# Two decoder layers on one core: the query projection is made from rows that carry only the norm's weights, and the token's factor comes in at the copy

## The reference

```python
def reference(...):
    for l in range(DEPTH):
        ...
        dp, st_p = mixer(rmsnorm(xp, norm_mix[l]), prm, None)
        ds, st_s = mixer(rmsnorm(xs, norm_mix[l]), prm, past)
        xp = xp + dp
        xs = xs + ds
        xp = xp + channel_mixer(rmsnorm(xp, norm_ffn[l]), l, ...)
...
def mixer(h, prm, past):
    (q, kc, vc, ks, vs, kw, vw, g_nsa, u, o_pre, if_pre, g_a, g_b) = split_cols(h @ prm['w_in'])
    q = q.reshape(b, t, NSA_KV_HEADS, NSA_GROUP, HEAD_DIM) * (HEAD_DIM ** -0.5)
    ...
    conv_prev = past['conv']
```

## Time and profile before

| what | us |
|---|---|
| median of 3 runs | 1853.33 (1851.79 to 1854.4) |
| the profiled execution, its own time | 1854.55 |
| its span in the profile | 1852.9 |
| TensorE busy in the span | 1746.0 (94%) |
| VectorE busy | 1035.3 (56%) |
| ScalarE busy | 810.8 (44%) |
| chain that ended last, share of TensorE | 85% |

### The profile page before, as it was taken

The page is one execution under the profiler, slowest core; times in us unless marked ns, Lnnn a source line. Parts: engine busy times, 40 slices in busy tenths (PEclk is TensorE's granted clock), DMA queues, the critical chain, the costliest instruction groups (busy, mean ns, idle before and its releaser), DMA issues.

```text
span 1852.9 us, 22952 instructions
## 1 busy us (share of the span) xinstructions
PE 1746.0 (94%) x8548; PEld 1394.4 (75%) x8548; DVE 1035.3 (56%) x1189; ACT 810.8 (44%) x873; POOL 176.7 (10%) x237
## 2 busy tenths in 40 slices
PE   6999979997999989998999899999999999999997
PEld 4567667777999956766776578888888888888875
DVE  2043421615454212343143468888888888888887
ACT  2013331114343110333120357777777767676764
POOL 2222011210000042201121010000000000000020
PEclk9999988998999989999899789999999999999999
DMA  8348323172554455521416389999999999999993
GB/s 239 122 156 253 112 67 93 52 229 63 165 180 163 90 163 183 159 69 58 103 46 214 134 301 332 401 351 400 356 402 350 400 352 403 352 395 360 393 391 122
DMA packets 230152, 424.92 MB, mean 229 GB/s; under 512 B 32414, under 2 KB 127934, under 8 KB 229884
## 3 DMA queue, kind: packets, MB, share of 16 engines
q1 hardware_dynamic: 217244, 383.62, 59.2%
q0 software_dynamic: 12832, 40.28, 6.6%
HBM read 403.70 MB, written 24.29 MB: 231 GB/s over the span
## 4 chain that ended last, share of the span: by engine, by line
PE 85%; DVE 6%; DMA 4%; ACT 2%; issue 2%; DVEq 0%; POOLq 0%; POOL 0%; SPq 0%; ACTq 0%
PE ps L717 81%; PE ps L721 4%; DMA weights_in<-in_moe_w 2%; DVE weights_low L1725 2%; DVE arena L1725 2%; ACT weights_high L1343 1%; DMA out_s_conv<-arena 1%; DVE arena L1912 1%; DMA arena<-in_cache_win 0%; DVE arena L1739 0%; DMA arena<-in_vecs 0%; POOLq L2415 0%; DMA arena<-in_state_conv 0%; DVE arena L1742 0%; DVE ffn_low L1725 0%
## 5 line engine op out<-in xcount | busy, mean ns | idle before, releaser
L717 PE MATMUL ps<-arena 128*128 128x288 f32 (+20 forms) x3180 | 719.9, 384 | 32.9 <-DMA arena<-in_vecs 8.9
L717 PEld LDWEIGHTS ps<-arena 128*128 128x128 f32 (+7 forms) x3180 | 508.9, 183 | 224.6 <-issue 91.5
L1725 DVE TENSOR_TENSOR weights_low<-weights_in,weights_high 128x3072 fp32r<-128x3072 f32 (+1 forms) x192 | 589.2, 3088 | 108.6 <-ACT weights_high L1343 108.4
L1343 ACT ACTIVATE weights_high<-weights_in 128x3072 fp32r<-128x3072 f32 (+1 forms) x192 | 489.6, 2560 | 200.2 <-PE ps L717 173.0
L717 PE MATMUL ps<-weights_high,item_high 128*128 128x512 f32 x704 | 279.2, 397 | 7.9 <-DVE weights_low L1725 7.2
L717 PE MATMUL ps<-weights_low,item_high 128*128 128x512 f32 x704 | 275.5, 391 | 0.0
L717 PE MATMUL ps<-weights_high,item_low 128*128 128x512 f32 x704 | 275.5, 391 | 0.0
L1340 ACT ACTIVATE arena<-arena 128x128 f32<-128x128 f32 (+12 forms) x188 | 74.9, 413 | 290.6 <-DVE arena L1725 95.8
L717 PEld LDWEIGHTS ps<-weights_high,item_high 128*128 128x128 f32 x704 | 133.3, 189 | 37.0 <-DVE weights_low L1725 9.6
L1343 ACT ACTIVATE arena<-ps 128x512 f32<-128x512 f32 (+16 forms) x146 | 63.3, 463 | 211.3 <-PE ps L721 136.6
L717 PEld LDWEIGHTS ps<-weights_high,item_low 128*128 128x128 f32 x704 | 133.1, 189 | 28.2
(11 more groups left out here) (182 smaller groups left out, 1438.1 us busy)
## 6 DMA issues: line engine op xcount, KB each, us to landing
weights_in<-in_moe_w SPq DMA_DIRECT2D x192, 768.0 KB, 8.1
weights_in<-in_moe_w SPq DMA_DIRECT2D x48, 1536.0 KB, 9.5
weights_in<-in_moe_w SPq DMA_DIRECT2D x64, 512.0 KB, 5.0
ffn_in<-in_ffn_w SPq DMA_DIRECT2D x30, 1024.0 KB, 7.1
weights_in<-in_moe_w SPq DMA_DIRECT2D x16, 1024.0 KB, 9.0
arena<-in_w_in SPq DMA_DIRECT2D x32, 384.0 KB, 4.0
arena<-in_w_in SPq DMA_DIRECT2D x32, 256.0 KB, 5.0
token_slots<-arena SPq DMA_DIRECT2D x12, 512.0 KB, 6.3
```

The source lines that it names most:

```text
L717: return nc.tensor.matmul(out, lhsT, rhs, start=start, stop=stop)
L1343: return nc.scalar.activation(out, x, ACT.Copy, scale=scale)
L1725: return V.tensor_tensor(out, x, y, op)
```

## The change

The query projection no longer reads `hT`. VectorE writes weighted rows `xg[k] = xT[k] * weight[k]`, without the token's factor, and TensorE makes the query tiles from them. The factor `srow` is multiplied in when VectorE, no longer ScalarE, copies the four query tiles out of PSUM. In layer 0 the eight weighted tiles are made just ahead of the norm, in layer 1 each one right after its residual addition at the end of the SwiGLU. On TensorE query tile 0 comes first, then the sums of the norm, then tiles 1 to 3, then the transposes of the convolution state, now into bank 7. The first key and value tile is what waits for `hT` now. ScalarE copies the state out after the square root, and takes the square root's table earlier by a one-column square root (`warm_m`): ahead of the squares in layer 0, after unit 33 for layer 1.

```diff
+        xg = take(KD * N, work0 + 2048).rearrange("p (k n) -> p k n", k=KD)
@@ tensor, start of a layer
-                pe.wait_ge(cvp_in.sem, cvp_in.at(l))
                 if l == 0:
                     pe.wait_ge(bp_ev.sem, bp_ev.at(0))
                     pe.wait_ge(vt_ev0.sem, vt_ev0.at(0))
                 else:
                     pe.wait_ge(fy_ev.sem, fy_ev.at(0))
-                for h in range(MH):
-                    m = tr(ps[:, 1, h * 24:h * 24 + 24], cvp[0:24, h * P:h * P + P])
-                m.then_inc(cv_pe.sem, 1)
-                norm(2 * l, 0 if l == 0 else KD - 2, KD)
-
                 pe.wait_ge(wl[0].sem, mixer_in(l, 0))
                 w = pslot(0, KD, 512)
                 for g in range(G):
                     if g == 1:
-                        pe.wait_ge(cv_ev.sem, cv_ev.at(l))
+                        norm(2 * l, 0 if l == 0 else KD - 2, KD)
                     for k in range(KD):
                         if g == 0:
-                            pe.wait_ge(h_ev.sem, h_ev.at(2 * l, k + 1))
-                        m = mm(ps[:, g, 0:N], w[:, k, g * P:g * P + P], hT[:, k, :], k == 0, k == KD - 1)
+                            pe.wait_ge(xg_ev.sem, xg_ev.at(l, k + 1))
+                        m = mm(ps[:, g, 0:N], w[:, k, g * P:g * P + P], xg[:, k, :], k == 0, k == KD - 1)
                     m.then_inc(q_pe.sem, 1)
+                pe.wait_ge(cvp_in.sem, cvp_in.at(l))
+                for h in range(MH):
+                    m = tr(ps[:, 7, h * 24:h * 24 + 24], cvp[0:24, h * P:h * P + P])
+                m.then_inc(cv_pe.sem, 1)
@@ tensor, key and value tiles
                         if b < 2:
                             pe.wait_ge(q_ev.sem, q_ev.at(l, b + 1))
+                        elif b == 7:
+                            pe.wait_ge(cv_ev.sem, cv_ev.at(l))
                         for k in range(KD):
+                            if f == 0 and m == 0:
+                                pe.wait_ge(h_ev.sem, h_ev.at(2 * l, k + 1))
@@ scalar, norm, after the square root
+                act.wait_ge(cv_pe.sem, cv_pe.at(idx // 2))
+                copy(uext[:, :, T + 3:UE].rearrange("p h (b x) -> p h b x", b=NB)[:, :, :, 0:3],
+                     ps[:, 7, 0:96].rearrange("p (h b x) -> p h b x", h=MH, b=NB)).then_inc(cv_ev.sem, 1)
@@ scalar, start of a layer
+                if l == 0:
+                    fn(warm_m, c("eps"), ACT.Sqrt)
                 norm(2 * l, fy_ev if l == 1 else None, 6 * l)
-                act.wait_ge(cv_pe.sem, cv_pe.at(l))
-                copy(uext[:, :, T + 3:UE].rearrange("p h (b x) -> p h b x", b=NB)[:, :, :, 0:3],
-                     ps[:, 1, 0:96].rearrange("p (h b x) -> p h b x", h=MH, b=NB)).then_inc(cv_ev.sem, 1)
-                for g in range(G):
-                    act.wait_ge(q_pe.sem, q_pe.at(l, g + 1))
-                    copy(qT[:, g, :], ps[:, g, 0:N], HD ** -0.5).then_inc(q_ev.sem, 1)
@@ scalar, end of layer 0's SwiGLU
                         unit_high(u)
+                        if u == 33:
+                            fn(warm_m, c("eps"), ACT.Sqrt)
@@ vector, start of a layer
+            def rows_weighted(l, k):
+
+                V.tensor_scalar(xg[:, k, :], xT[:, k, :], vT[:, V_MIX + 8 * l + k:V_MIX + 8 * l + k + 1], None, ALU.mult
+                                ).then_inc(xg_ev.sem, 1)
+
             for l in range(2):
                 dve.wait_ge(vt_ev0.sem, vt_ev0.at(0))
+                if l == 0:
+                    for k in range(KD):
+                        dve.wait_ge(xt_ev.sem, xt_ev.at(0, k + 1))
+                        rows_weighted(0, k)
                 norm(2 * l, V_MIX + 8 * l)
+                for g in range(G):
+                    dve.wait_ge(q_pe.sem, q_pe.at(l, g + 1))
+                    V.scalar_tensor_tensor(out=qT[:, g, :], in0=ps[:, g, 0:N], scalar=HD ** -0.5, in1=srow,
+                                           op0=ALU.mult, op1=ALU.mult).then_inc(q_ev.sem, 1)
@@ vector, end of layer 0's SwiGLU, tiles 0 to 5 and again tiles 6 and 7
                                 tt(xT[:, d, :], xT[:, d, :], ps[:, YBANK[d % 4], 0:N], ALU.add).then_inc(fy_ev.sem, 1)
+                                dve.drain()
+                                rows_weighted(1, d)
```

More of the change, by code:

```diff
@@ L401, in build @@
         cvp_in, cmp_in = ev("conv_in", 16), ev("cmp_in", 16 * 34)
[L402 to L406, removed]
+        q_pe, cv_pe, kv_pe, u_pe, o_pe, if_pe, ct_pe, kt_pe, hid_pe, mqk_pe, kc_pe = ev("mixer_tensor", 41).steps(
+            4, 1, 6, 4, 4, 1, 9, 1, 2, 8, 1)
+        xg_ev, q_ev, kv_ev, u_ev, cst_ev, uc_d, if_ev, qz_ev = ev("mixer_vector", 26).steps(8, 4, 6, 4, 1, 1, 1, 1)
+        cv_ev, gs_ev, o_ev, uc_a, ct_a, kt_ev, lf_a, lf_a2, row_a, hid_ev, kc_a = ev("mixer_scalar", 19).steps(
+            1, 1, 4, 1, 5, 1, 1, 1, 1, 2, 1)
         lf_d, ct_d, lf_d2, row_d, c_ev, mqk_ev, hidr_ev, kc_d = ev("compress_vector", 19).steps(1, 4, 1, 1, 2, 8, 1, 1)
@@ L2136, in _ @@
                         tt(xT[:, d, :], xT[:, d, :], ps[:, YBANK[d % 4], 0:N], ALU.add).then_inc(fy_ev.sem, 1)
-                    dve.drain()
+                        dve.drain()
+                        rows_weighted(1, d)
                 else:
```

## The result

The changed kernel's median was 1839.8 us (1834.14 to 1843.34, four executions) against 1853.87: a ratio of 0.9923, 95% interval 0.9896 to 0.9950. It is faster, by 14.1 us where 18.5 were forecast, and the median stands 0.3 us above the stated range. The profiled execution was the fastest of the four, 1834.14. Three more calls timed the same kernel: 1837.0, 1836.95 and 1839.51, six executions each, against medians of the kernel before of 1854.12, 1854.55 and 1855.52 in the same calls. So the gain was 14.1, 17.1, 17.6 and 16.0 us by call, and the median of all 22 executions is 1838.3. Eight of the 22 lie above 1839.5, the upper end of the range.

What follows compares the result with a forecast made beforehand. TensorE was taken to bound the kernel, losing time to waits and slow clock at both layers' starts. Gains 5.4 + 13.1 = 18.5 us gave 1836.05 for the profiled execution, 1834.8 against the median; range 1831.5 to 1839.5.

Steps and rivals of the forecast that it cites:

- The bound and the place: TensorE, 85% of the chain; its waits at both layers' starts: normed tiles 7.5 us, convolution state 5.8 us.
- rivals 2 and 3: Window cache waits: layer 0's gain ends there, 1840.2, 8%; or both layers' gains do, no change, 1853.3, 4%.
- Rival 4: Layer 1's start: query weights arrive late, beyond a 1.8 us margin; slower past 18.5 us of lateness; 3%.
- Rival 5: Layer 1's first matmul still waits for `fy_ev`, so the 5.1 us would stay: 1839.9; no chance of its own.
- Layer 1, 13.1 us: SwiGLU's end to first key matmul, 678.24 to 665.1: 3.76 pause, 5.1 transfer, rest slow clock.
- Layer 0, 5.4 us: Layer 0's start: first key matmul moves from 60.36 to 55.0, a gain of 5.4 us.
- 55.0: Layer 0's first key matmul: start 35.2, then 3.88 tile 0, 3.88 sums, 11.64 tiles 1 to 3, 0.40 transposes.
- my 0.42: Weighted tile on VectorE: 0.42 us, taken between rows of 0.406 (one operand) and 0.511 (two operands).
- Parts at nothing: Both layers: norm chain, four query copies on VectorE, SwiGLU's weighted tiles and earlier table load cost nothing, being covered.
- The sum: 18.5: Both layers' starts: 5.4 + 13.1 = 18.5 us, carried to the end unchanged.
- with 1.5 us either way for the spread between runs (2.6 us before): Whole kernel: margin around the forecast 1834.8, also for half-clock stretches elsewhere that shift; the forecast had 70%.
- the clock rival: Layer 0's start: clock falls all the same as the pause grows from 1.99 to about 2.6; costs up to 1.96 us; 15%.

## Why the prediction was partly right

**The bound and the place: right.** The waits named are the ones that went, and only they. The window cache's waits stayed at 9 us each, so rivals 2 and 3 fall. Rival 4 falls: the first query matmul of layer 1 starts 0.51 us after the addition begins, so the weights were there. Rival 5 falls with it. (Rival 4's price for a landing at 670 us comes to 1856.6, not 1856: 1834.8 + 670 - 648.24.)

**Layer 1, 13.1 us: right.** Start to first key copy went from 36.0 to 23.2, which is 12.7 us unrounded, and it is 23.2 in all four profiles of the full change; alone layer 1 gave 13.8 on the median.

**Layer 0, 5.4 us: right in mechanism, 5.0 in size, less when the clock falls.** Alone it gave 4.5 on the median. From the end of the setup's matmuls (32.64 before, 33.13 after) to the first key copy it took 33.0 us before and 28.0 after, so 5.0; the same 28.0 stands in the three profiles of the full change that held the clock, and 29.4 in the one where it fell. From weighted tile to key matmul the pair of profiles shows 35.62 + 19.64 + 0.35 = 55.6 where I had 55.0; the setup itself ended half a microsecond later in that execution. The weighted tile took 0.33 us on the path and 0.371 on the mean, under my 0.42 and its lower end of 0.406.

**Parts at nothing: right.** Norm chain, query copies (0.452 against 0.454), weighted tiles and table load stayed under cover; the copies' last one ends 5.5 us before VectorE's next work.

**The sum: 18.5, a little too large; measured 14.1 at first and 16 to 17.6 later.** The two starts give 5.0 + 12.7 = 17.7 in the profiles. The missing 0.8 lies in two terms. The prediction took the start of ScalarE's copy (60.36, 678.24) for the first key matmul; the records of the kernel before have 396-column matmuls from 60.1 and 678.0 on, so each gain was counted 0.2 us too large. And a query tile takes 3.93 us (19.64 / 5), not 3.88. From 17.7 to the full change's pooled 16.2 (1854.5 less 1838.3) or, by means, 16.8 (1854.8 less 1838.0) no second cost was found, and none is needed: resampling the 65 and 22 executions puts the medians' difference between 14.5 and 18.9 us. In one profile of four the fall at layer 0's start takes 1.4 us. Elsewhere the pieces move both ways: layer 1's mixer has 389.1 to 393.3 us against 390.1 before, the experts and the end 773.6 to 779.4 against 777.0 and 779.2, and the fastest of the four executions has a mixer of 392.3. How much of the last microsecond the change brings and how much is chance is open.

**What failed is the step "with 1.5 us either way for the spread between runs (2.6 us before)".** Three executions stood for the spread. Calls with 21, 17, 11 and 11 executions of the kernel before spread over 11.5, 8.9, 8.1 and 10.2 us, and the changed kernel over 9 in its first four. The same three executions set the base of the sum, 1853.33, where 65 executions have 1854.5: the forecast stood 1.2 us low by that, and 2.3 by a gain of 16.2 in place of 18.5. So the changed kernel's centre, 1838.3, is 3.5 us above 1834.8, inside the range but near its upper end. Medians of four drawn from the 22 executions go from 1834.6 to 1841.5 in 95 of 100 draws, and about one in four lies above 1839.5. That the first one did is bad luck; that it could is the failed step. The same step left the clock rival too small: 15% and 1.96 us, against three falls in six profiles with the new pause (one in four of the full change), of up to 3.0 us. Its reason, that the pause grows from 2.0 to 2.6 us, is not borne out: the clock fell after the old pause too, in two of five. The Trainium skill (TensorE: Matmul & The Clock Gate, Part 1) says of its own measurements that the point of change varies from run to run. I cited it for the rival's direction and didn't draw its consequence for the range.

## What to carry to other kernels

A factor of the token can be taken out of the moving rows and put in where the tile is copied out of PSUM: the matmuls then start without the norm, and the norm's chain hides under them. Look for a second wait in front of the same place (here the state's transfer), since each alone gave about 6 us of the 12.7. And before setting a range, look at more than three executions, and ask of every short pause in the profile whether the clock only happened to hold.

## What the runs showed of the hardware that was not expected

- TensorE's clock fell to 1.2 GHz during or after pauses of 1.94 to 2.5 us in some executions and held in others of the same kernel; and it fell after some 4 us of matmuls with 15 columns during which the records show no pause. A fall at layer 0's start cost 1.4, 1.7 and 3.0 us up to the first key copy.
- Matmuls whose result nobody reads, 12 in one pause and 10 in each of two others, went with a kernel about 5 us faster, from 1838.3 to 1832.9 on the medians of 22 and 10 executions, in part from different calls.
- The weighted tiles come every 0.30 us (eight in 2.44 us), against 0.44 for the two-operand form on the same columns. GpSimd's issues of the cache pages beside them kept their pace: the pairs of issues start at 34.71 and 36.45 in the changed kernel, 1.74 us apart, and at 34.22 and 35.97, 1.75 us apart, in the kernel before, which has no weighted tiles there:

```profile
34.71 1.27 POOL L2450 DMA_DIRECT2D arena<-in_cache_cmp  x2 [26.77 <-issue]
36.45 1.24 POOL L2450 DMA_DIRECT2D arena<-in_cache_cmp  x2 [0.47 <-issue]
38.17 1.22 POOL L2450 DMA_DIRECT2D arena<-in_cache_cmp  x2 [0.48 <-issue]
```

The third pair, begun when VectorE had finished its eight tiles at 37.5, comes 1.72 us after the second. The Trainium skill (SBUF — State Buffer, "SBUF: two separate sides") warns that GpSimd can't write its descriptors while VectorE runs an instruction in a mode that uses two ports. No run here shows in which mode the weighted tiles ran, so this neither confirms nor contradicts the page: no delay of GpSimd shows beside them.
